# Two feed-forward stages with first and second products taken in pairs of chunks

## The reference, cut to what matters

```python
for layer in range(2):
    ...                                   # a token mixer and its residual
    h = modulate(rms_norm(x, norm_g[layer, 2]), sh2, sc2)
    y = square(relu(h @ ff_w_in[layer])) @ ff_w_out[layer]   # 1024 -> 4096 -> 1024
    x = x + g2 * rms_norm(y, norm_g[layer, 3])
```

## Time and profile before

| what | value |
|---|---|
| time, median of 3 runs | 1004.23 us (1004.12 to 1004.72) |
| time of the profiled execution | 1004.23 us |
| its span (first to last instruction) | 1002.2 us |
| around the span | 2.0 us |
| TensorE matmul busy | 977.6 us, 98% of the span |
| VectorE busy | 800.3 us, 80% |
| ScalarE busy | 539.6 us, 54% |
| GpSimd busy | 77.4 us, 8% |
| mean granted TensorE clock | 0.998 of full speed |

### The profile page before, as it was taken

One profiled execution on the slowest core, in us unless ns is written; L12 is line 12 of the kernel. 1 busy time (PEld: TensorE's weight loads), 2 busy tenths in 40 slices (PEclk: granted clock), 3 DMA queues, 4 the chain that ended last, 5 costly groups with the idle time before them and its releaser, 6 DMA issues.

```text
span 1002.2 us, 17008 instructions
## 1 busy us (share of the span) xinstructions
PE 977.6 (98%) x6941; PEld 858.0 (86%) x6941; DVE 800.3 (80%) x1208; ACT 539.6 (54%) x706; POOL 77.4 (8%) x80
## 2 busy tenths in 40 slices
PE   6999999999999999999999999999999999999997
PEld 3587799989987999886889999988999789999996
DVE  1449799858998988887978778873799789888896
ACT  4354554444447557765546454464765665554544
POOL 0000000000000000000640000000691000000000
PEclk9999999999999999999999999999999999999999
DMA  9999699969997997014998777735334376555511
GB/s 338 388 383 378 219 335 394 360 232 359 347 340 260 278 372 293 2 43 128 385 368 308 280 273 286 256 93 169 127 131 128 121 269 235 176 203 184 195 43 43
DMA packets 130333, 243.62 MB, mean 243 GB/s; under 512 B 6586, under 2 KB 95311, under 8 KB 124111
## 3 DMA queue, kind: packets, MB, share of 16 engines
q1 hardware_dynamic: 125616, 238.77, 67.5%
q10 hardware_dynamic: 4639, 3.76, 1.4%
HBM read 239.37 MB, written 1.05 MB: 240 GB/s over the span
## 4 chain that ended last, share of the span: by engine, by line
PE 78%; DVE 7%; POOL 4%; ACT 3%; DMA 3%; issue 2%; SPq 2%; POOLq 0%; DVEq 0%; ACTq 0%
PE bank L2052 25%; PE bank L1984 12%; PE bank L1985 12%; PE bank L1986 12%; DMA raw<-in_a_w_in_dram 3%; PE bank L2064 2%; PE bank L2337 1%; DVE wlo L1202 1%; PE bank L2363 1%; PE bank L1876 1%; ACT t L778 1%; POOL eb L2719 1%; PE bank L2375 1%; DVE hcat L1347 1%; PE bank L1898 1%
## 5 line engine op out<-in xcount | busy, mean ns | idle before, releaser
L1202 DVE TENSOR_TENSOR wlo<-raw,whi 128x2048 fp32r<-128x2048 f32 x143 | 327.1, 2293 | 48.3 <-ACT whi L727 47.2
L727 ACT ACTIVATE whi<-raw 128x2048 fp32r<-128x2048 f32 x144 | 274.2, 1905 | 130.9 <-PE bank L2052 65.7
L1984 PE MATMUL bank<-hcat,whi 128*128 128x256 f32 x1096 | 309.2, 282 | 0.7 <-DVE wlo L1202 0.7
L1985 PE MATMUL bank<-hcat,whi 128*128 128x256 f32 x1096 | 303.7, 277 | 0.0
L1986 PE MATMUL bank<-hcat,wlo 128*128 128x256 f32 x1096 | 303.5, 277 | 0.0
L1984 PEld LDWEIGHTS bank<-hcat,whi 128*128 128x128 f32 x1096 | 206.5, 188 | 7.3 <-issue 3.0
L1985 PEld LDWEIGHTS bank<-hcat,whi 128*128 128x128 f32 x1096 | 206.1, 188 | 1.4
L1986 PEld LDWEIGHTS bank<-hcat,wlo 128*128 128x128 f32 x1096 | 206.1, 188 | 0.0
L1829 DVE SCALAR_TENSOR_TENSOR cvt<-ut,vec,cvt 128x189 f32<-128x189 f32 (+2 forms) x176 | 68.2, 429 | 17.5 <-ACT cvt L1165 15.1
L2052 PE MATMUL bank<-whi,fhi 128*128 128x512 f32 x240 | 74.9, 393 | 0.0
L2052 PE MATMUL bank<-wlo,fhi 128*128 128x512 f32 x240 | 74.1, 390 | 0.0
(11 more groups left out here) (434 smaller groups left out, 1655.2 us busy)
## 6 DMA issues: line engine op xcount, KB each, us to landing
raw<-in_ada_w_dram SPq DMA_DIRECT2D x40, 1024.0 KB, 8.8
raw<-in_ff_w_in_dram SPq DMA_DIRECT2D x32, 1024.0 KB, 7.9
raw<-in_ff_w_out_dram SPq DMA_DIRECT2D x32, 1024.0 KB, 7.5
raw<-in_w_ada_dram SPq DMA_DIRECT2D x24, 1024.0 KB, 5.8
raw<-in_w_up_dram SPq DMA_DIRECT2D x22, 1024.0 KB, 5.2
raw<-in_w_in_dram SPq DMA_DIRECT2D x12, 1024.0 KB, 5.8
raw<-in_w_down_dram SPq DMA_DIRECT2D x11, 1024.0 KB, 5.1
raw<-in_ada_w_dram SPq DMA_DIRECT2D x16, 512.0 KB, 12.0
```

What stands on the lines that cost most here:

```text
L727: act.activation(whi[:, m % SPL, 0:w], raw[:, pl.nm[m] % RAW, 0:w], ACT.Copy).then_inc(s_hi, 1)
L1202: dve.tensor_tensor(wlo[:, m % SPL, 0:w], raw[:, pl.nm[m] % RAW, 0:w], whi[:, m % SPL, 0:w], ALU.subtract).then_inc(s_lo, 1)
L1984: pe.matmul(dst, wh[:, kt, n], ah[:, kt, :], start=kt == 0, stop=False)
L1985: pe.matmul(dst, wh[:, kt, n], al[:, kt, :], start=False, stop=False)
```

## The change

In both feed-forward stages the chunks are taken in pairs. TensorE's order becomes u0, u1 u2, d0 d1, u3 u4, d2 d3, ... u13 u14, d12 d13, u15, d14 d15. The list of loads follows that order: u0, u1, u2, d0, its ada chunks, d1, its ada chunks, u3, u4, d2, ... The functions `ff_up`, `ff_down` and `ff_splits` give the new places of the weights; all waits and splittings use them. The small matmul with zeros stays only in the first of each two first products (odd c). On ScalarE the copies of finished modulation rows (`ada_row`) move a little so that they stand between the right splittings. Everything else stays.

```diff
         M_FF[f] = pl.m(cols(win, 0))
-        pl.m(cols(win, 256))
         for c in range(16):
+            if c % 2 == 0:
+                for d in range(c + 1, min(c + 3, 16)):
+                    pl.m(cols(win, 256 * d))
             pl.m(rows(wout, 2 * c), 0)
             ada_loads(FF_ADA[f][c])
-            if c < 14:
-                pl.m(cols(win, 256 * (c + 2)))
+    def ff_up(c):
+        return max(0, 2 * c - 2 + c % 2)
+    def ff_down(c):
+        return min(2 * c + 3 - c % 2, c + 16)
+    def ff_splits(c):
+        return 2 * c + 4 - c % 2
...
-                    m = m0 + (2 * c - 1 if c else 0)
-                    act.wait_ge(s_mm, m + 1)
+                    act.wait_ge(s_mm, m0 + ff_up(c) + 1)
...
                     epi(c)
+                    if c == 14:
+                        splits(m0 + ff_splits(c) - 2)
                     if c >= 14:
                         gain_row(u, c - 14)
-                    splits(m0 + min(2 * c + 4, 33))
-                    if ends_at(f, c - 1) is not None:
-                        ada_row(ends_at(f, c - 1))
+                    if c % 2 == 0 and ends_at(f, c - 2) is not None:
+                        splits(m0 + ff_splits(c) - 1)
+                        ada_row(ends_at(f, c - 2))
+                    splits(m0 + ff_splits(c))
+                    if c == 15:
+                        ada_row(ends_at(f, 14))
...
-                        dve.wait_ge(s_mm, m0 + 2 * (c - 3) + 3)
+                        dve.wait_ge(s_mm, m0 + ff_down(c - 3) + 1)
...
-                    splits(m0 + min(2 * c + 4, 33))
+                    splits(m0 + ff_splits(c))
...
-                    linear_mid(m0 + (2 * c - 1 if c else 0), hh, hl, o=o, zeros_at=(0, 2))
+                    linear_mid(m0 + ff_up(c), hh, hl, o=o, zeros_at=(0, 2) if c % 2 else None)
...
-                    ff_in(c + 1)
+                    if c % 2 == 0:
+                        for d in range(c + 1, min(c + 3, 16)):
+                            ff_in(d)
...
-                        rows_onto_y(m0 + 2 * c + 2, *squares(c), first=c == 0)
+                        rows_onto_y(m0 + ff_down(c), *squares(c), first=c == 0)
```

## The result

The kernel after took 1007.36 us at the median (1005.33 to 1008.30, 15 executions) against 1004.58 us (1004.12 to 1006.14, 15 executions) for the kernel before: 1.0022 times as long, 95% interval 1.0015 to 1.0029. Two more timings on other chips gave 1.0009 (1.0000 to 1.0018) and 1.0012 (1.0002 to 1.0023). The change costs between 0.1 and 0.2%; it was forecast to win 0.5 us.

The account below looks back on a forecast made before the run. TensorE, busy for 98% of the span, was taken to bound the kernel alone. Gain and waits, -2.4 + 1.5 + 0.4 = -0.5 us, took 1004.23 to 1003.7 us, with a range of 1001.6 to 1005.2.

Parts of the forecast that it names:

- What TensorE gains: First products in both feed-forward stages: the second of each pair runs faster, 0.17 us a pair, 14 pairs, 2.4 us won.
- The waits in ffn0: TensorE waits for VectorE's low parts: u5 1.10 us, u3 and u11 0.04 each, plus 0.3 in all; 1.5 us lost.
- ffn1's first pair: Wait for u3's low part in ffn1, with VectorE operations longer beside GpSimd's masks: 0.4 us, between 0 and 1.1.
- (13, 14): Pair u13, u14 of ffn0: VectorE's window 15.61 us and some 0.8 more, against 16.36 plus 0.45; no wait.
- No wait appears: Rival: TensorE gets no new wait in the feed-forward stages; -2.4 to -2.6 us, 1001.7 us; chance 0.16.
- nothing gained: Rival: the second first-product block still takes 5.61 us and waits of 1.9 us come; 1006.1 us; chance 0.08.
- the second block slow throughout: Rival: without its own zeros the second first product keeps 0.118 us a matmul; +2.6 us, 1006.8 us; chance 0.06.
- VectorE blocked by GpSimd: Rival: in ffn1's first pair VectorE waits for a whole GpSimd instruction; +3.0 us, 1007.2 us; chance 0.05.
- Loads late: Rival: the DMA, nearly full in ffn0, has nothing to catch up with; 1 us more, 1004.7 us; chance 0.03.

## Why the prediction was wrong

The forecast was 1003.7 us and "no difference that can be told"; the result lies 3.7 us above, outside the range of 1001.6 to 1005.2. So does the median at the higher clock, 1005.72. Of the 3.7 us, 1.6 come from two terms of the sum, a wait that it had at nothing and one that it had too small; most of the rest goes with the clock, for which the sum had no term.

- **What TensorE gains: right.** 0.17 a pair forecast, 0.185 measured; 14 times 2.6 for 2.4. The reading of the earlier trace rows, that the second of two first products runs at 0.113 a matmul, held. By the Trainium skill, TensorE: Matmul & The Clock Gate, section Back-to-back issue gap, the order would win next to nothing (the section gives its formula for single matmuls and says that a stream with weight loads differs); here one and the same matmul has two paces, and the trace decides.
- **The waits in ffn0: right.** u5 1.24 for 1.20, u3 0.19 and u11 0.23 for 0.14 each, no others among the pairs. The sum over VectorE's operations against 16.36 us of TensorE worked, and VectorE idles ahead of odd epilogues as forecast (0.86 us ahead of epi(1), 2.12 ahead of epi(3)).
- **ffn1's first pair: mis-sized.** 0.4 forecast, 1.05 measured. The term took the bounds 0 and 1.1 and then chose 0.4, "as only some of the operations there are longer": from the low part at 499.56 on all of them were, by 1.37 us up to the low part of u3 and by 0.58 in it, and the kernel with the masks moved shows that the wait doesn't come without them. The right value was near the bound. The Trainium skill, SBUF - State Buffer, section Who interferes with whom, says that a VectorE operation with two inputs in SBUF contends with a GpSimd one that reads SBUF, under an exclusive lock; the rows agree that they collide, and the most that one `lo` grew by is 0.62 us. Whether one stops for a whole instruction of the other they don't show.
- **The end of ffn0: the step that failed.** The forecast stood "(13, 14) ... none", and "u0, u1, u15 and the last products keep their neighbours". That asked whether u15's low part comes in time, which it did. It did not ask who waits for epi(15), behind everything that the shifted order pushes back on VectorE: d15 does, with the row sums ahead of it, 0.97 us where the forecast had none. The trace of before showed it without any slack, with 0.05 us from the end of the last epilogue to the row sums. The run with the moved chunks and the chunk of d14 moved shows that this chunk's place is enough to remove the wait.
- **The clock: a term that was missing.** The terms above give -2.6 + 1.66 + 1.05 + 0.97 = +1.1 for the forecast -0.5, and the executions at the higher clock show +1.10. The sum took 1004.23 for its base, an execution without a fall of the clock, where 45 of the 91 of the kernel before whose clock is known had the lower clock. The remaining 1.7 us of the first medians go with the clock: the first 15 executions of the kernel after had the lower one 11 times, where 22 of all 37 had it, and it cost them 1.8 us where it cost the kernel before 1.5. The shares 22 of 37 and 45 of 91 don't show that the change alters how often the clock falls, but the lowest means do suggest it: 0.995 or less stands in none of the 91, in 3 of the 37 and in 12 of the 72 executions of the six other kernels with pairs. What would bring a second fall, in u0, where TensorE's order is unchanged, no run shows.
- **The rivals.** "No wait appears" did not happen (u5, 0.98). Nor did "nothing gained" and "the second block slow throughout"; the run without zeros shows that the latter would have, in eight of 14 pairs, had the first block lost its zeros too. "VectorE blocked by GpSimd" named the right place, with 3.5 us above the forecast where 0.65 came. "Loads late" did not happen: every new wait of TensorE ends on VectorE.

## What to carry to other kernels

When an order is changed by hand, the engine that follows must be walked through to the end of the stage, not only to the next block: the slack of each wait of before (here none at the end of ffn0) says where a shift of 1 us comes out. A gain in the fastest engine's own blocks is kept only if the engine behind it is shifted as well; here the pairs won 2.6 us, gave 3.7 back in five waits, and the same pairs with two moves in the list of loads keep all 2.6. Where a term has a bound from rows in which two engines disturb one another, take the bound if they overlap for the whole stretch. And a time with two levels needs a base with both: a median of three executions can miss one of them.

## What the runs showed of the hardware

- A first product of 48 matmuls (256 columns) behind 512-column matmuls runs at 0.118 us a matmul to its end, and the next one too, at a granted clock of 1.00; one small matmul with zeros, or a low part that comes late for the block, brings it to 0.113. The pair without zeros took 11.31 us undisturbed, 11.00 to 11.02 behind waits of 0.50 to 0.99, and 10.89 where only the first weight load was late.
- The granted clock falls from 1.00 to 0.50, the lower level of 1.2 GHz, for some 3 us, in attention and in some kernels with pairs in u0 of ffn0 too. About half the executions of either kernel have a mean clock of 0.997 or less (45 of 91 of the kernel before, 22 of 37 of the kernel after), at a price of 1.5 and 1.8 us by the medians. In the two microseconds before the fall in attention that is shown TensorE is busy for 2.00 of 2.00 us, with matmuls of 65 and 128 columns. TensorE stays busy throughout, and the clock rises again. No run here shows why it falls in one execution and not in the next.
